# Conditioning product by rows on VectorE in place of partial sums finished on TensorE

## The chip, the cores and the metric

The kernel runs on one core of one Trainium2 chip. The metric is the device time of one execution in microseconds (us). All tensors are float32.

## The reference

The program is a chain of four transformer-like blocks over one sequence of 512 tokens with 1024 features. What matters here is the conditioning ("modulation") of the first two blocks:

```
mod = (silu(c) @ ada_w + ada_b).reshape(bsz, DEPTH, 2, 3, D_MODEL)   # c: 1 x 1024, ada_w: 1024 x 12288
...
shift, scale, gate = (mod[:, i, 0, k][:, None, :] for k in range(3))
h = rmsnorm(x, norm_g[i, 0]) * (1.0 + scale) + shift
y = short_conv_mixer(h, ...)            # i = 0: h @ w_in (1024 x 3072), products, a convolution, @ w_out
x = x + gate * rmsnorm(y, norm_g[i, 1])
shift, scale, gate = (mod[:, i, 1, k][:, None, :] for k in range(3))
h = rmsnorm(x, norm_g[i, 2]) * (1.0 + scale) + shift
y = swiglu_ffn(h, f_w_in[i], f_w_out[i])
x = x + gate * rmsnorm(y, norm_g[i, 3])
```

So `mod` is 12288 numbers, each a dot product of length 1024: 12.6 million multiply-adds over 50 MB of weights. The first 2048 of them (shift and scale of the first norm) are needed before the first large matmul can start.

## The kernel before, in words

Features lie on the 128 partitions, tokens on the free axis: `x` is 8 k tiles of 128 x 512. Every large matmul is done as three float32r products, with the weight chunk `raw` (128 x 1024) split into `whi` (ScalarE, `split_hi`, L1104) and `wlo` (GpSimd, `split_lo`, L518), and the activations into `h_hi` and `h_lo`. A ring of four chunks (`RING = 4`) is loaded by the SyncE queue; SP reloads a slot when `lo_ready` says that its `wlo` is done.

The phases come in program order: `a_in` (24 chunks of 24 matmuls each), `a_out` (8), `f_in0` (44), `f_out0`, then the state-space mixer `m`, `f_in1` and `f_out1` (the same shape of work as `f_in0` and `f_out0`), attention, and a last feed-forward. Each engine runs its own instruction list in the order in which the code is written; semaphores join them.

At the start of a phase, `four` computes the first four output tiles k tile by k tile, so that TensorE can begin as soon as k tile 0 of the normalised input is there (L580 for the two products with `h_hi`, L584 for the one with `h_lo`). All other chunks go through `chunk` (L557).

The normalised input of k tile k is made by three engines. VectorE multiplies `x` by the inverse root, which `spread` has laid over a PSUM bank (`scaled`, L1598, into one of two buffers `ta`; from k = 2 on it waits for the ScalarE work on tile k-2). ScalarE applies scale and shift twice (`norm_out`, L1149 to `h_hi`, L1150 to `tb`). GpSimd, for the last tile VectorE, subtracts (`h_lo`, L533, L1565).

The modulation is made in 24 units of 512 outputs. VectorE adds up, over the 8 k tiles, weight times SiLU(c), with the contraction on the partitions (`mod_unit` L1662 to L1671, `first_part` L1682 to L1687: one `tensor_scalar` and seven `scalar_tensor_tensor` of 128 x 512 each, summed in a PSUM bank, the last one into `modacc` or `acc`). TensorE then sums over the partitions with a column of ones (`modulation` L669, `first_sum` L681 and L685: four float32 matmuls of 128 x 1, which the trace shows as eight), and VectorE adds the bias (`mod_evac` L1654, `first_cols` L1698). Units 0 to 3 are the first stage (`ada_first`). Units 4 to 11 come in `a_in`, one behind each of its eight column groups (`ada_a`), and units 12 to 23 in `f_in0` (`ada_f`). `modulation` stands 20 times in TensorE's list: six times in `a_in`, once in `a_out`, 13 times in `f_in0`.

## Time and profile before

| | |
|---|---|
| median of 3 runs | 2212.21 us (2212.01 to 2213.32) |
| profiled execution, span from first to last instruction | 2209.9 us |
| median less span of the profiled execution | 2.3 us |
| TensorE busy | 2167.0 us, 98% |
| VectorE busy | 1203.4 us, 54% |
| ScalarE busy | 999.4 us, 45% |
| GpSimd busy | 973.0 us, 44% |

No device time of the profiled execution itself is given apart from its span; the other runs last 2.3 us longer than that span. The profile's rows are in microseconds from the start of the span unless marked ns. A row of the timeline gives start, duration, engine, line, operation, and in brackets how long the engine was idle before it and what released it.

### The profile page before, as it was taken

The numbers are of one execution on the slowest core, as the hardware profiler recorded it, in microseconds if no ns is written. First come the engines' busy times: TensorE is split into PE (matmuls) and PEld (weight loads), VectorE is DVE, ScalarE is ACT, GpSimd is POOL, SyncE is SP. The second block draws the span as 40 slices with busy tenths as digits, with TensorE's granted clock in tenths as the row PEclk, the third lists the DMA queues.
The fourth block names the chain that finished last, engine by engine and source line by source line (L and its number), as shares of the span: only waits on it lengthen the run. The fifth ranks groups of instructions, "written<-read, shape, count | busy, mean of one in ns | idle before, by whom it ended". The sixth has DMA issues, their size and how long they took to land.

```text
span 2209.9 us, 29015 instructions
## 1 busy us (share of the span) xinstructions
PE 2167.0 (98%) x10456; PEld 1756.4 (79%) x10456; DVE 1203.4 (54%) x1720; ACT 999.4 (45%) x1425; POOL 973.0 (44%) x421
## 2 busy tenths in 40 slices
PE   7999999999999999999999999999999899999998
PEld 5788888888878777778888888888777688888886
DVE  5877665521176877886522221240888755666522
ACT  4324544334445655654543434453555644444332
POOL 3544444446644333334544456666122143444563
PEclk8999999999999999999999999999999999999999
DMA  7653475553315344333232323344221132333232
GB/s 316 221 209 124 147 272 218 178 161 97 115 58 194 115 148 157 115 124 96 77 95 95 96 74 101 109 122 155 87 70 42 36 105 86 104 95 95 79 97 72
DMA packets 74338, 273.88 MB, mean 124 GB/s; under 512 B 8632, under 2 KB 11320, under 8 KB 67849
## 3 DMA queue, kind: packets, MB, share of 16 engines
q1 hardware_dynamic: 70872, 266.77, 36.5%
q10 hardware_dynamic: 3376, 5.90, 0.8%
q8 instruction: 58, 0.95, 0.2%
q14 instruction: 32, 0.25, 0.0%
HBM read 269.24 MB, written 8.12 MB: 126 GB/s over the span
## 4 chain that ended last, share of the span: by engine, by line
PE 76%; issue 14%; POOL 5%; DVE 3%; ACT 1%; DMA 1%; ACTq 0%; SPq 0%; POOLq 0%; DVEq 0%
PE bank L557 61%; POOL wlo L518 5%; PE bank L974 4%; PE bank L1066 2%; PE bank L580 2%; PE bank L1031 1%; PE bank L995 1%; PE bank L622 1%; PE bank L1014 1%; PE bank L584 1%; PE bank L630 1%; PE bank L669 1%; DMA ada_first<-ada_d 1%; DVE x L1624 1%; PE bank L915 1%
## 5 line engine op out<-in xcount | busy, mean ns | idle before, releaser
L518 POOL TENSOR_TENSOR wlo<-raw,whi 128x1024 fp32r<-128x1024 f32 x382 | 927.6, 2435 | 1146.7 <-ACT whi L1104 1146.4
L1104 ACT ACTIVATE whi<-raw 128x1024 fp32r<-128x1024 f32 x382 | 400.5, 1055 | 560.3 <-PE bank L557 537.8
L557 PE MATMUL bank<-h_hi,whi 128*128 128x512 f32 x1608 | 633.0, 394 | 1.9 <-POOL wlo L518 1.9
L557 PE MATMUL bank<-h_hi,wlo 128*128 128x512 f32 x1608 | 626.5, 390 | 0.0
L557 PE MATMUL bank<-h_lo,whi 128*128 128x512 f32 x1608 | 625.8, 389 | 0.0
L557 PEld LDWEIGHTS bank<-h_hi,whi 128*128 128x128 f32 x1608 | 301.9, 188 | 68.3 <-issue 6.3
L557 PEld LDWEIGHTS bank<-h_hi,wlo 128*128 128x128 f32 x1608 | 301.8, 188 | 64.0
L557 PEld LDWEIGHTS bank<-h_lo,whi 128*128 128x128 f32 x1608 | 302.0, 188 | 61.6
L557 PE MATMUL bank<-g_hi,whi 128*128 128x512 f32 x592 | 230.4, 389 | 0.0
L557 PE MATMUL bank<-g_hi,wlo 128*128 128x512 f32 x592 | 230.3, 389 | 0.0
L557 PE MATMUL bank<-g_lo,whi 128*128 128x512 f32 x592 | 230.3, 389 | 0.0
L1786 DVE TENSOR_TENSOR tb<-ta,bank 128x512 f32<-128x512 f32 x44 | 30.2, 686 | 210.4 <-PE bank L557 193.6
L1565 DVE TENSOR_TENSOR g_lo<-tb,g_hi 128x512 f32 (+1 forms) x52 | 108.3, 2082 | 51.9 <-ACT g_hi L1236 45.0
L557 PEld LDWEIGHTS bank<-g_lo,whi 128*128 128x128 f32 x592 | 111.1, 188 | 23.1
L557 PEld LDWEIGHTS bank<-g_hi,wlo 128*128 128x128 f32 x592 | 111.1, 188 | 23.1
L557 PEld LDWEIGHTS bank<-g_hi,whi 128*128 128x128 f32 x592 | 111.1, 188 | 23.0
L1581 DVE TENSOR_TENSOR sums<-sums,sq 128x512 f32<-128x512 f32 x21 | 14.5, 692 | 186.2 <-ACT sq L1167 186.1
L1724 DVE SCALAR_TENSOR_TENSOR tb<-bank,vec,tb 128x511 f32<-128x511 f32 (+1 forms) x140 | 104.9, 749 | 9.8
L580 PE MATMUL bank<-h_hi,whi 128*128 128x512 f32 x160 | 66.4, 415 | 9.8 <-ACT h_hi L1149 9.8
L533 POOL TENSOR_TENSOR h_lo<-tb,h_hi 128x512 fp32r<-128x512 f32 x35 | 45.2, 1293 | 65.6 <-ACT tb L1150 65.3
L580 PE MATMUL bank<-h_hi,wlo 128*128 128x512 f32 x160 | 65.5, 409 | 0.0
L2156 DVE TENSOR_TENSOR x<-x,bank 128x512 f32<-128x512 f32 x8 | 5.5, 688 | 86.4 <-PE bank L557 86.4
(357 smaller groups left out, 2985.2 us busy)
## 6 DMA issues: line engine op xcount, KB each, us to landing
raw<-f_in_d SPq DMA_DIRECT2D x88, 512.0 KB, 3.5
raw<-m_d SPq DMA_DIRECT2D x65, 512.0 KB, 3.6
ada_f<-ada_d SPq DMA_DIRECT2D x24, 1024.0 KB, 7.0
raw<-g_in_d SPq DMA_DIRECT2D x44, 512.0 KB, 3.5
raw<-w_in_d SPq DMA_DIRECT2D x41, 512.0 KB, 3.6
csb<-cs_d SPq DMA_DIRECT2D x32, 640.0 KB, 6.3
ada_a<-ada_d SPq DMA_DIRECT2D x16, 1024.0 KB, 4.9
raw<-a_in_d SPq DMA_DIRECT2D x24, 512.0 KB, 6.0
```

Source lines behind the costliest of these rows:

```text
L518: nc.gpsimd.tensor_tensor(wlo[:, s], raw[:, s], whi[:, s].bitcast(F32), ALU.subtract).then_inc(lo_ready, 1)
L533: nc.gpsimd.tensor_tensor(h_lo[:, k, :], tb[:, k % 2, :], h_hi[:, k, :].bitcast(F32), ALU.subtract).then_inc(in_ready, 1)
L557: mm = nc.tensor.matmul(psum[bank][:], w[:, s, kk, :], xs[part == "lo"][:, k, :], start=first and kk == 0 and i == 0, stop=last and kk == ...
L580: nc.tensor.matmul(psum[tiles[i]][:], w[:, (C0[name] + i) % RING, k, :], h_hi[:, k, :], start=k == 0 and j == 0, stop=False)
L584: mm = nc.tensor.matmul(psum[tiles[i]][:], whi[:, (C0[name] + i) % RING, k, :], h_lo[:, k, :], start=False, stop=k == KD - 1)
L622: mm = nc.tensor.matmul(psum[bank][:, i:i + 1], src[:, i * P:(i + 1) * P], ones[:, 0:1], start=start and i == 0, stop=False, skip_group_ch ...
L974: mm = nc.tensor.matmul(psum[7][:], w[:, c % RING, m // 3, :], (h_hi, h_lo)[part == "lo"][:, m // 3, :], start=m == 0, stop=m == 23)
L1066: mm = nc.tensor.matmul(psum[b][:], w[:, c % RING, k, :], (h_hi, h_lo)[part == "lo"][:, k, :], start=kk == 0 and i == 0, stop=kk == 3 and ...
L1104: nc.scalar.activation(whi[:, s], raw[:, s], ACT.Copy).then_inc(hi_ready, 1)
L1565: TT(dst, whole, hi.bitcast(F32), ALU.subtract).then_inc(in_ready, 1)
L1724: ins = STT(out=out[:, d:S], in0=src[:, 0:S - d], scalar=col(width - 1 - d), in1=out[:, d:S], op0=ALU.mult, op1=ALU.add)
L1786: TT(tb[:, j % 2, :], ta[:, j % 2, :], psum[b][:], ALU.mult).then_inc(bank_free[b], 1)
```

## The change

The contraction goes to the free axis. `c` is loaded broadcast over all partitions (`cond`, 128 x 1024), ScalarE takes its SiLU into two PSUM banks (`silu_c`, banks 6 and 7), and the weights `ada_w` are stored transposed, so that one partition holds all 1024 weights of one output. One instruction, `tensor_tensor_reduce` over 128 x 1024 (`mod_col`), multiplies, sums, adds the bias and writes one column of `mod`: 128 outputs. A unit is four such instructions. No matmul is left for the modulation. The bytes that are loaded stay the same but for `cond`.

The first stage goes by k tile: shift column k and scale column k, then `scaled(k)`. The mean square of `x` is summed on VectorE (seven additions) in place of eight matmuls with ones. In the SyncE queue the order of the first loads changes, and in ScalarE's list all four `split_hi` of the first ring stand together in front of the first norm. Since banks 6 and 7 are needed by the residual step after `a_out`, the SiLU is made a second time in front of `f_in0` (`condition()`).

```diff
-        acc = sb("acc", [P, S])
-        modacc = sb("modacc", [P, S])
+        cond = sb("cond", [P, 2, S])
+        acc, spare = cond[:, 0, :], cond[:, 1, :]
...
+        silu_c = banks[:, 6:8, :]
...
-                for h in range(2):
-                    dst = ada_first[p][:, 4 * h:4 * h + 4].rearrange("p k n -> p (k n)")
-                    sp.dma_start(dst, io["ada"][2 * p + h]).then_inc(first_in[p][h], 16)
-
-            sp.dma_start(vec[:], io["vec"]).then_inc(vec_in, 16)
+                    sp.dma_start(ring[h].rearrange("p e a n -> p (e a n)"), at(io["ada"], 2 * d + h + it * (2 * n))).then_inc(ada_in[h], 16)
+
+            def ada_start(k):
+                sp.dma_start(ada_first[k].rearrange("p e a n -> p (e a n)"), io["ada"][k]).then_inc(first_in[k], 16)
+
             for h in range(2):
                 sp.dma_start(x[:, 4 * h:4 * h + 4], io["x"].rearrange("p (k n) -> p k n", k=KD)[:, 4 * h:4 * h + 4]).then_inc(x_in[h], 16)
+            sp.dma_start(cond[:].rearrange("p a n -> p (a n)"), io["c"].broadcast_to([P, D])).then_inc(c_in, 16)
+            sp.dma_start(vec[:], io["vec"]).then_inc(vec_in, 16)
+            ada_start(0)
             sp.dma_start(kst[:], io["kst"]).then_inc(kst_in, 16)
-            for v in range(2):
+            load(io["a_in"][0], 0)
+            ada_start(1)
+            for v in range(1, 4):
                 load(io["a_in"][v], v)
-            ada_start(0)
-            for v in range(2, 4):
-                load(io["a_in"][v], v)
-            for p in range(1, 4):
-                ada_start(p)
...
                     turn(k, range(4))
-                    if n == 0 and k % 2 == 0:
-                        first_sum(1 + k // 2)
...
             def first_root():
 
-                for k in range(KD):
-                    pe.wait_ge(sq_out, k + 1)
-                    nc.tensor.matmul(psum[4][:], ones[:], sq[:, k % 2, :], start=k == 0, stop=k == KD - 1).then_inc(row_done, 1)
-                pe.wait_ge(row_out, 1)
-                for i in range(NT):
-                    mm = nc.tensor.matmul(psum[4][:, i:i + 1], rstd[0:1, i * P:(i + 1) * P], ones[0:1, 0:1], start=True, stop=True)
-                mm.then_inc(s_done, 1)
...
-            def modulation(i):
...
+                pe.wait_ge(row_acc, KD - 1)
+                token_sums(4, rstd[:], True).then_inc(s_done, 1)
...
             first_root()
-            first_sum(0)
...
@@ -696,8 +661,6 @@
                 for s in range(3):
                     if 3 * j + s >= 4:
                         single("a_in", 3 * j + s)
-                    if j >= 2 and s == 0:
-                        modulation(2 + j)
                 if j < 3:
 
...
                 single("a_out", u, xs=(g_hi, g_lo))
-                if u == 0:
-                    modulation(10)
             residual_roots(0, sums)
 
             def ffn(n):
-                if n == 0:
-                    four("f_in0", 1)
-                    modulation(11)
+                four(f"f_in{n}", 1 + 2 * n)
+                with pe.Fori(0, 10) as it:
                     for u in range(4, 8):
-                        single("f_in0", u, wait=False)
...
-                    modulation(23)
...
+                        single(f"f_in{n}", u, it, 4, wait=False)
...
-                        act.wait_ge(ncol_ready, k // 2 + 1)
+                        act.wait_ge(ncol_ready, k + 1)
...
 
-            act.wait_ge(vec_in, 16)
-            nc.scalar.activation(csil[:], vec[:, V0["c"]:V0["c"] + KD], ACT.Silu).then_inc(csil_ready, 1)
+            def condition():
+
+                nc.scalar.activation(silu_c, cond[:], ACT.Silu).then_inc(c_ready, 1)
+
             act.wait_ge(const_ready, 1)
+            nc.scalar.activation(root[:, SPARE, 0:1], epscol[:], ACT.Silu)
             for k in range(KD):
                 if k % 4 == 0:
                     act.wait_ge(x_in[k // 4], 16)
-                if k >= 2:
-                    act.wait_ge(row_done, k - 1)
-                nc.scalar.activation(sq[:, k % 2, :], x[:, k, :], ACT.Square).then_inc(sq_out, 1)
-                if k >= KD - 2:
-                    split_hi(k - (KD - 2))
-            act.wait_ge(row_done, KD)
-            nc.scalar.activation(rstd[0:1, :], psum[4][0:1, :], ACT.Copy).then_inc(row_out, 1)
+                if k >= 3:
+                    act.wait_ge(row_acc, k - 2)
+                nc.scalar.activation(sq[:, k % 2, :] if k else rstd[:], x[:, k, :], ACT.Square).then_inc(sq_out, 1)
+            act.wait_ge(c_in, 16)
+            condition()
             set_root()
-            split_hi(2)
-            act.wait_ge(s_ready, 1)
-            take_root(0, ssum[:])
-            split_hi(3)
+            act.wait_ge(s_done, 1)
+            take_root(0, psum[4][:, 0:NT])
+            for c in range(RING):
+                split_hi(c)
+            act.wait_ge(vec_in, 16)
             mod_norm(0, "a_in", 0)
 
...
+            act.wait_ge(ncol_ready, KD + 1)
             mod_norm(1, "f_in0", 1)
+            condition()
...
+            def mod_col(t, src):
+
+                return nc.vector.tensor_tensor_reduce(src, src, silu_c, 1.0, V("ada_b", t), ALU.mult, ALU.add, mod[:, t:t + 1])
+
+            def mod_unit(d, ring):
+
+                for h in range(2):
+                    dve.wait_ge(ada_in[h], 16 * (d - 3))
+                    for e in range(2):
+                        ins = mod_col(4 * d + 2 * h + e, ring[h][:, e])
+                    ins.then_inc((ada_half, mod_part)[h], 1)
+
+            def first_cols(k):
+
+                ins = mod_col(KD + k, ada_first[k][:, 1])
+                ins.then_inc(col_out, 1)
+                dve.wait_ge(col_out, k + 1)
+                ins = STT(out=ncol[:, 0, 0, k:k + 1], in0=mod[:, KD + k:KD + k + 1], scalar=1.0, in1=V("norm_g", k), op0=ALU.add, op1=ALU.mult)
+                ins.then_inc(ncol_ready, 1)
...
+            for k in range(1, KD):
+                dve.wait_ge(sq_out, k + 1)
+                if k >= 2:
+                    dve.wait_ge(row_acc, k - 1)
+                TT(rstd[:], rstd[:], sq[:, k % 2, :], ALU.add).then_inc(row_acc, 1)
...
+            dve.wait_ge(c_ready, 1)
+            for k in range(KD):
+                dve.wait_ge(first_in[k], 16)
+                ins = mod_col(k, ada_first[k][:, 0])
+                if k == 0:
+                    dve.wait_ge(std_out, 1)
+                    nc.vector.tensor_copy(ssum[:], psum[4][:, 0:NT])
                     inverse(0, R1)
+                first_cols(k)
+                if k == 0:
                     dve.wait_ge(rb_done, 1)
...
+                scaled(k, 4, 0, "a_in")
             low("a_in")
...
+                    dve.wait_ge(c_ready, 2)
+                    for j in range(KF):
+                        hidden(j)
+                        if j % 4 < 3 and j < 16:
+                            mod_unit(12 + 3 * (j // 4) + j % 4, ada_f)
+                        if j == 15:
+                            dve.wait_ge(mod_part, 20)
+                            gate_col(1)
+                            for q in range(2, 4):
+                                scale_col(q)
+                                gate_col(q)
...
-    order = [c for p in range(4) for c in (2 * p, 2 * p + 1, 8 + 2 * p, 9 + 2 * p)] + list(range(16, 96))
-    ada = a["ada_w"].reshape(2, KD // 2, P, 96, P)[:, :, :, order]
-    ins["ada"] = ada.reshape(2, KD // 2, P, 24, S).transpose(3, 0, 2, 1, 4).reshape(48, P, KD // 2 * S)
+    ins["c"] = a["c"]
+    order = [t for k in range(KD) for t in (k, KD + k)] + list(range(2 * KD, 96))
+    ins["ada"] = a["ada_w"].T.reshape(96, P, D)[order].reshape(48, 2, P, D).transpose(0, 2, 1, 3).reshape(48, P, 2 * D)
```

Left out are the deleted bodies of `modulation`, `first_sum`, `mod_evac`, `first_part` and the old `mod_unit` and `first_cols`, which the print above has.

What stands in VectorE's list in the first stage, before: from the end of unit 0's partial sum to the middle of unit 1's. `ssum` gets the mean squares, `ta` is the output of `scaled`, and a unit covers two k tiles of shift and scale.

```order
L1687 SCALAR_TENSOR_TENSOR modacc<-ada_first,csil,bank 128x512 [waits dve_step]
L1744 COPY ssum<-bank 128x4 [waits s_done]
L1682 TENSOR_SCALAR bank<-ada_first,csil 128x512 [waits first_in1_0]
L1687 SCALAR_TENSOR_TENSOR bank<-ada_first,csil,bank 128x512 [waits dve_step] x3
L1698 TENSOR_TENSOR mod<-bank,vec 128x2x2 [waits mod_sum,dve_step]
L1702 SCALAR_TENSOR_TENSOR ncol<-mod,vec 128x2 [waits mod_out]
L1570 RECIPROCAL root<-root 128x4 [waits std_out]
L1598 TENSOR_TENSOR ta<-x,bank 128x512 [waits rb_done,r_ready]
L1598 TENSOR_TENSOR ta<-x,bank 128x512
L1687 SCALAR_TENSOR_TENSOR bank<-ada_first,csil,bank 128x512 [waits first_in1_1]
L1687 SCALAR_TENSOR_TENSOR bank<-ada_first,csil,bank 128x512 [waits dve_step] x2
```

In the change, the same place: from the shift column of k tile 0 to `scaled(1)`. The first of each pair of ISA rows is the multiply-and-sum of 128 x 1024, the second writes the sum to one column of `mod` (128 x 1).

```order
L1597 ISA mod 128x1
L1656 COPY ssum<-bank 128x4 [waits std_out]
L1517 RECIPROCAL root<-root 128x4 [waits std_out]
L1597 ISA ada_first,mod<-ada_first,bank,vec 128x1024 [waits r_ready]
L1597 ISA mod 128x1
L1612 SCALAR_TENSOR_TENSOR ncol<-mod,vec 128x1 [waits col_out]
L1545 TENSOR_TENSOR ta<-x,bank 128x512 [waits rb_done]
L1597 ISA ada_first,mod<-ada_first,bank,vec 128x1024 [waits first_in1]
L1597 ISA mod 128x1
L1597 ISA ada_first,mod<-ada_first,bank,vec 128x1024
L1597 ISA mod 128x1
L1612 SCALAR_TENSOR_TENSOR ncol<-mod,vec 128x1 [waits col_out]
```

The eight instructions for two k tiles with a wait for TensorE's sum (`mod_sum`) became two instructions for each k tile with no wait on TensorE, and `scaled` comes once per k tile instead of twice per unit.

ScalarE's list in front of the first norm, before: L1194 squares `x`, L1104 is `split_hi`, L1115 takes the root.

```order
L1104 ACTIVATE whi<-raw 128x1024 [waits raw_in0]
L1194 ACTIVATE sq<-x 128x512 [waits row_done]
L1104 ACTIVATE whi<-raw 128x1024 [waits raw_in1]
L1198 ACTIVATE rstd<-bank 1x512 [waits row_done]
L1119 ACT_TABLE_LOAD
L1119 ACTIVATE root<-epscol 128x1
L1104 ACTIVATE whi<-raw 128x1024 [waits raw_in2]
L1115 ACTIVATE root<-ssum,epscol 128x4 [waits s_ready]
L1104 ACTIVATE whi<-raw 128x1024 [waits raw_in3]
L1149 ACTIVATE h_hi<-ta,mod,ncol 128x512 [waits t_out,ncol_ready]
```

In the change (L1132 is the SiLU of `cond`, L1059 the root, L1048 `split_hi`, L1093 the first `h_hi`):

```order
L1141 ACTIVATE sq<-x 128x512 [waits row_acc] x3
L1132 ACTIVATE bank<-cond 128x1024 [waits c_in]
L1063 ACT_TABLE_LOAD
L1063 ACTIVATE root<-epscol 128x1
L1059 ACTIVATE root<-bank,epscol 128x4 [waits s_done]
L1048 ACTIVATE whi<-raw 128x1024 [waits raw_in0]
L1048 ACTIVATE whi<-raw 128x1024 [waits raw_in1]
L1048 ACTIVATE whi<-raw 128x1024 [waits raw_in2]
L1048 ACTIVATE whi<-raw 128x1024 [waits raw_in3]
L1093 ACTIVATE h_hi<-ta,mod,ncol 128x512 [waits t_out,ncol_ready,vec_in]
```

The splits of chunks 0 and 1 moved behind the squares, and all four splits now stand between the root and the first norm.

SyncE's loads, before:

```order
L384 DMA vec<-vec_d 128x616
L386 DMA x<-x_d 128x2048 x2
L387 DMA kst<-kst_d 128x262
L363 DMA raw<-a_in_d 128x1024 x2
L382 DMA ada_first<-ada_d 128x2048 x2
L363 DMA raw<-a_in_d 128x1024 x2
L382 DMA ada_first<-ada_d 128x2048 x6
L395 DMA dtp<-dtp_d 128x64
```

and in the change:

```order
L380 DMA x<-x_d 128x2048 x2
L381 DMA cond<-c_d 128x1024
L382 DMA vec<-vec_d 128x608
L377 DMA ada_first<-ada_d 128x2048
L384 DMA kst<-kst_d 128x262
L358 DMA raw<-a_in_d 128x1024
L377 DMA ada_first<-ada_d 128x2048
L358 DMA raw<-a_in_d 128x1024
L377 DMA ada_first<-ada_d 128x2048
L358 DMA raw<-a_in_d 128x1024
L377 DMA ada_first<-ada_d 128x2048
L358 DMA raw<-a_in_d 128x1024
L377 DMA ada_first<-ada_d 128x2048 x4
```

Chunk 3 of `raw` was the tenth load, behind two loads of `ada_first` (1024 KB each); now it is the thirteenth, behind four of them and `cond` (512 KB). Before, `vec` is 308 KB, each of the two loads of `x` 1024 KB, `kst` 131 KB and a chunk of `raw` 512 KB.

## Rows read from the trace of the kernel before

**Rows 1.** The page, part 1: busy time, share of span, instructions.

```profile
PE 2167.0 (98%) x10456; PEld 1756.4 (79%) x10456; DVE 1203.4 (54%) x1720; ACT 999.4 (45%) x1425; POOL 973.0 (44%) x421
```

**Rows 2.** What TensorE waited for, whole span: total us, times, longest.

```profile
PE bank L580 <- ACT h_hi L1149: 9.8, 6, 2.1
...
PE bank L669 <- DVE modacc L1671: 1.0, 1, 1.0
```

**Rows 3.** Chain that ended last, a_in: start us, us, what.

```profile
130.12 0.79 PE bank L669 x8
130.90 16.49 PE bank L557 x72
```

**Rows 4.** The same chain at starts and ends of both feed-forwards.

```profile
232.61 3.11 PE bank L580 x8
...
607.26 4.36 PE bank L622 x40
...
1085.72 337.58 PE bank L557 x1488
...
1423.30 4.36 PE bank L622 x40
```

**Rows 5.** TensorE's timeline at the start of f_in1.

```profile
1061.38 0.47 PE L580 MATMUL bank<-h_hi,whi 128*128 128x512 f32 x1 [1.82 <-ACT h_hi L1149]
```

**Rows 6.** The same chain in the first stage.

```profile
6.00 15.85 DMA ada_first<-ada_d
...
28.56 0.82 ACT h_hi L1149
...
29.43 3.78 PE bank L580 x8
33.21 1.71 PE bank L584 x4
...
58.59 0.96 PE bank L708 x2
```

**Rows 7.** Windows: length, busy PE, PEld, DVE, ACT, POOL, clock, DMA share, GB/s.

```profile
10.00:15.00 5.00, 5.00 (x11) 1.72 (x9) 0.42 (x1) 2.87 (x6) 0.00 (x0) 1.00 1.02 430
...
25.00:30.00 5.00, 2.62 (x9) 2.28 (x10) 2.60 (x7) 1.44 (x3) 0.33 (x1) 0.50 1.01 428
```

**Rows 8.** VectorE by group and shape: busy us, mean ns, idle before.

```profile
L1935 DVE TENSOR_TENSOR csb<-csb,cbm 128x1280 f32<-128x1280 f32 x32 | 47.5, 1491 | 4.7 <-ACT cbm L1284 2.2 <-ACT csb L1276 1.6
...
L1898 DVE RECIPROCAL rstd<-rstd 128x512 f32<-128x512 f32 x8 | 26.8, 3345 | 1.9 <-ACT rstd L1292 1.9
...
L1687 DVE SCALAR_TENSOR_TENSOR bank<-ada_first,csil,bank 128x512 f32<-128x512 f32 x22 | 16.6, 755 | 0.7
...
L1761 DVE TENSOR_TENSOR ta<-ta,bank 128x512 f32<-128x512 f32 x8 | 5.4, 681 | 2.8 <-ACT ta L1211 2.8
```

**Rows 9.** VectorE's timeline, two neighbours of a few elements.

```profile
424.32 0.17 DVE L1716 TENSOR_TENSOR ncol<-mod,vec 128x8 f32<-128x8 f32 x1
424.40 0.16 DVE L1709 SCALAR_TENSOR_TENSOR ncol<-mod,vec 128x8 f32<-128x8 f32 x1
```

**Rows 10.** VectorE's timeline, one column group of a_in.

```profile
154.49 0.68 DVE L1761 TENSOR_TENSOR ta<-ta,bank 128x512 f32<-128x512 f32 x1
...
160.93 2.48 DVE L1565 TENSOR_TENSOR g_lo<-tb,g_hi 128x512 fp32r<-128x512 f32 x1 [0.92 <-ACT g_hi L1219]
165.48 0.16 DVE L1654 TENSOR_TENSOR mod<-bank,vec 128x4 f32<-128x4 f32 x1 [2.08 <-PE bank L669]
...
171.76 0.68 DVE L1761 TENSOR_TENSOR ta<-ta,bank 128x512 f32<-128x512 f32 x1
```

**Rows 11.** VectorE's timeline, one tile of f_in0.

```profile
396.47 0.69 DVE L1786 TENSOR_TENSOR tb<-ta,bank 128x512 f32<-128x512 f32 x1 [1.48 <-PE bank L557]
398.22 2.33 DVE L1565 TENSOR_TENSOR g_lo<-tb,g_hi 128x512 f32 x1 [1.06 <-ACT g_hi L1236]
```

**Rows 12.** ScalarE's timeline between f_in0's norm and its first split.

```profile
253.34 1.06 ACT L1104 ACTIVATE whi<-raw 128x1024 fp32r<-128x1024 f32 x1 [2.99 <-PE bank L584]
```

More of the change, by code:

```diff
@@ L174, in program @@
         sums = view(H + 16 * KB, "sums", [P, 3, S])
[L176 to L178 removed]
+        ada_a = [view(at, f"ada_a{i}", [P, 2, 2, S]) for i, at in enumerate((G + 16 * KB, G + 24 * KB))]
+        ada_first = [view(G + 8 * KB * k, f"ada_first{k}", [P, 2, 2, S]) for k in range(KD)]
+        ada_f = [view(at, f"ada_f{i}", [P, 2, 2, S]) for i, at in enumerate((G + 36 * KB, G + 80 * KB))]
         y32 = view(G + 44 * KB, "y32", [P, 16, S])
@@ L203, in program @@
         tbias = [view(at, f"tbias{i}", [P, 2, TB]) for i, at in enumerate((G + 73 * KB, G + 64 * KB))]
-        abias = [t[:].rearrange("p (e w) -> p e w", e=2) for t in (modacc, acc)]
+        abias = [t[:].rearrange("p (e w) -> p e w", e=2) for t in (spare, acc)]
         kc2 = view(G + 73 * KB, "kc2", [P, 2, 2, S])
@@ L707, in _ @@
                     e = min(S, WB + WA - S * j)
[L708 removed]
+                    nc.tensor.matmul(psum[5][0:16, 0:e], tbl[:], hot[:, S * j:S * j + e], start=True, stop=True).then_inc(hot_sum, 1)
             for u in range(KD):
                 single("a_out", u, xs=(g_hi, g_lo))
[L711 to L712 removed]
             residual_roots(0, sums)
             def ffn(n):
[L716 to L718 removed]
+                four(f"f_in{n}", 1 + 2 * n)
+                with pe.Fori(0, 10) as it:
                     for u in range(4, 8):
[L720 to L736 removed]
+                        single(f"f_in{n}", u, it, 4, wait=False)
                 with pe.Fori(0, 2) as it:
@@ L1677, in first_part @@
-            def first_part(p, h):
-                out, half = psum[6 + p % 2][:], KD // 2
-                dve.wait_ge(first_in[p][h], 16)
-                if h == 0:
-                    step(TS(out, ada_first[p][:, 0, :], csil[:, 0:1], None, ALU.mult))
-                elif p >= 2:
-                    dve.wait_ge(mod_sum, p - 1)
-                end = KD if p else DIRECT[0]
-                for k in range(max(1, half * h), min(half * (h + 1), end)):
-                    ins = STT(out=out if k < end - 1 else (modacc, acc)[p % 2][:], in0=ada_first[p][:, k, :], scalar=csil[:, k:k + 1],
-                              in1=out, op0=ALU.mult, op1=ALU.add)
-                    if k < end - 1:
-                        step(ins)
-                if h:
-                    ins.then_inc(mod_part, 1)
@@ L2229, in layout @@
     ins = {}
-    vecs = dict(c=columns(a["c"]), ada_b=columns(a["ada_b"]), norm_g=columns(a["norm_g"]),
+    vecs = dict(ada_b=columns(a["ada_b"]), norm_g=columns(a["norm_g"]),
                 a_conv=taps_columns(a["a_conv_w"][0]),
```

145 lines of the change are left out of this document (19 added, 126 removed).

## The prediction

> **What bounds the kernel now.** I read the page's busy times first: TensorE is busy for 2167.0 of 2209.9 us, and no other engine passes 54% [rows 1]. A busy engine that is pipelined need not be at its peak, so next comes what TensorE waited for. There is almost nothing outside the first stage and attention: 9.8 us in six waits over the whole span for the first tiles of the norms, none longer than 2.1, and one wait of 1.0 us for `modacc` [rows 2]. So from the end of the first stage to the end of `f_out0` (607 us) each microsecond of TensorE's own list is a microsecond of the kernel, and each one off VectorE is worth nothing unless it ends a wait. The chain of waits shows the same in `a_in`: 72 matmuls in 16.49 us, a modulation in 0.79, and so on without a gap [rows 3].
>
> The first stage is the exception. Its chain goes through loads of `ada_first` (one lands at 6.00 + 15.85 = 21.85 us), then VectorE's sums, and the four first tiles start at 29.43 and are over at 58.59 [rows 6]. The 96 matmuls of these tiles need 96 x 0.227 = 21.8 us at the pace of `f_in1` (337.58 us for 1488) [rows 4], so some 37 of these 58.6 us are something else.
>
> **The change part by part.**
>
> *Twenty modulations off TensorE.* In `a_in` a period with one of them is 0.79 + 16.49 = 17.28 us [rows 3]; 72 matmuls at 0.227 us would be 16.34. The difference is 0.94 us: 0.79 for the small matmuls and 0.15 for the change to and from them. Seven of them (six in `a_in`, one in `a_out`) make 6.6 us. For the 13 in `f_in0` the kernel has its own control, since `f_in1` is the same work without modulation. From the first L580 to the residual sums `f_in0` takes 607.26 - 232.61 = 374.65 us, and `f_in1` 1423.30 - 1061.38 = 361.92 [rows 4, 5]. That is 12.7 us, with the wait of 1.0 us for `modacc` in it, and with whatever `f_in1` waits for when no small matmul covers it. Sum: **19.3 us**. Bounds: 18.2, if the change to and from them costs nothing in `a_in` (7 x 0.79 + 12.7), and 19.8 (20 x 0.94 + 1.0).
>
> *The price of one column.* The trace has no multiply-and-sum. VectorE's operations with one operand in PSUM take 681 ns for 512 elements, and a product of 1280 elements takes 1491 ns [rows 8]; that is 1.05 ns for each further element, so 1.22 us for 1024. A second arithmetic step costs no second pass: `scalar_tensor_tensor` of 512 elements takes 755 ns [rows 8]. The write of the sum is an instruction of its own in VectorE's list; its nearest rows are operations of 8 columns, which take 0.17 us but follow each other at 0.08 [rows 9]. I take 1.22 + 0.08 = 1.30 us for a column. The lower bound is 1.15 + 0.08, if neighbours overlap as those of rows 9 do. The upper one, by the nearest row in kind of a slow single instruction, is RECIPROCAL with 3345 ns for 512 elements [rows 8]; between such ends I stay near the additions and products, since the sum is an addition per element, but I keep half rate (2 x 1.07, and 0.15 that does not grow with the size, = 2.3 us, 2.4 with the write) as a case.
>
> The Trainium skill speaks on this point ("Vector Engine (DVE) Microarchitecture Reference", section "Points that are easy to get wrong"): an instruction of the scalar_tensor_tensor layout with an accumulator runs at half throughput when both sources are float32 in SBUF. Here one of them (`silu_c`) is in PSUM, so by its words it would not apply; if it did apply, each column would be about 2.3 us. No row of before shows either.
>
> *Units in `a_in` and `f_in0`.* A unit is now 4 x 1.30 = 5.2 us in place of 171.76 - 165.48 = 6.3 [rows 10]. The rest of a column group in `a_in` is 160.93 + 2.48 - 154.49 = 8.9 us, so VectorE has 14.1 us of work in a period of 16.3 [rows 10, 3]; in `f_in0` a tile is 398.22 + 2.33 - 396.47 = 4.1 us [rows 11] and with a unit 9.3 in 10.9 (48 matmuls). All of it lies beside TensorE's work: 0 us. The cover is gone at 7.4 us a unit in `a_in` (1.8 a column). ScalarE's second SiLU (128 x 1024) costs about what a split of the same size costs, 1.06 us, and stands where ScalarE was idle for 2.99 us [rows 12]: 0 us, at most 1 if more than that came late.
>
> *The first stage.* What is late next? In ScalarE's list all four splits stand ahead of the first norm, and the last one needs chunk 3 of `raw`. Up to it, the queue holds `x` 2048 KB, `cond` 512, `vec` 304, four `ada_first` 4096, `kst` 131 and four chunks 2048: 9139 KB. Before, the load that landed at 21.85 us had 7607 KB up to its end (308 + 2048 + 131 + 4 x 512 + 3 x 1024) [rows 6]. The loads flow at 428 to 430 GB/s from 10 us on [rows 7], so 1532 KB (1.57 MB) more are 3.7 us: chunk 3 lands at **25.5 us**. The squares, seven additions, the SiLU, the root and the columns of k tiles 0 and 1 are done before that (about 21 us: `ada_first` 1 lands near 17, two columns and a `scaled` follow), so they cost nothing; they have some 4 us of cover. Behind the waiting split stand the first norm and thereby `scaled(2)`, which waits for `tb` of tile 0.
>
> Split 3 ends at 26.6. The first `h_hi` takes 0.82 us [rows 6], so TensorE starts at 27.5 in place of 29.43. From there two chains run. TensorE: k tile 0 at the low clock (granted 0.50 of 2.4 GHz, that is 1.2 GHz, as it was when it began before [rows 7]) is 3.78 + 1.71 = 5.5 us [rows 6], the other 84 matmuls 19.1, and 0.5 for the clock's rise: 52.6. VectorE: `tb` of tile 0 is out at 28.2, `scaled(2)` ends at 28.9, and each further k tile is 2 x 1.30 + 0.2 (the scale column's wait and its small operation) + 0.69 = 3.5 us, so `scaled(7)` ends at 46.4. Then come 0.8 + 0.8 us of ScalarE, 0.7 of VectorE's `h_lo` and the last 14 matmuls (3.3): 52.0. The two are within a microsecond of each other, and I take 52.6 against 58.59: **6.0 us** less. Bounds: with columns of 1.23 us TensorE's chain still holds (52.6); with the clock low for one more k tile it is 55; with 1.30 us more per k tile (a collision, below) it is 58.5. An earlier end than 51 would need the clock to rise at once.
>
> Sum: 19.3 + 6.0 = 25.3 us off the span of 2209.9. The median lay 2.3 us above that span, and I expect the same distance: 2212.2 - 25.3 = **2187 us**.
>
> **The rivals.**
>
> *Full forecast* (2187, chance 0.70). Own range 2182 to 2191.
>
> *VectorE's columns collide with GpSimd* (2193, chance 0.12). `h_lo` at 160.93 took 2.48 us [rows 10], while a subtraction of 128 x 512 elements otherwise takes about what the product in rows 8 takes: it waits while GpSimd splits. If a column waited likewise, each k tile of the first stage would gain GpSimd's 1.3 us for its own `h_lo` and end at 58.5, no better than before. In `a_in` a unit could catch one more split (1.8 us): 15.9 of 16.3, still covered. So 19.3 is left: 2193. For it speaks that the instruction writes its whole product to SBUF; against it, that rows of L1687 with a PSUM operand stay at 755 ns while GpSimd works [rows 8]. The Trainium skill ("SBUF — State Buffer", section "Who interferes with whom") has it that an instruction with at most one SBUF input does not contend; L1687's rows agree, for another operation.
>
> *Chunk 3 lands late, or the clock stays low* (2190 to 2192, chance 0.06, taken with the case before in the range). `cond` is a broadcast, 128 times the same 4 KB; each microsecond it takes above its share comes off the 6.0.
>
> *Half rate, which ends on the other side* (2216, chance 0.09). At 2.4 us a column the first stage has k tiles of 5.7 us: 28.9 + 28.5 + 5.6 = 63, or 4.4 us later than now. In `a_in` VectorE needs 8.9 + 9.6 = 18.5 us in 16.3: 2.2 x 8 = 17.6 us. In `f_in0` it is (3 x 13.7 + 4.1) / 4 = 11.3 in 10.9, 0.4 x 16 = 6. Together 28 against 19.3: 9 us slower, or 4 if the first groups are covered by slack, so 2216 to 2221. The sign turns at about 2.2 us a column.
>
> *The matmuls go and nothing is gained* (2206 to 2212, chance 0.03). TensorE would have to wait for something that the small matmuls hid. Against it stands `f_in1`, which runs the same list without them and is 12.7 us shorter.
>
> **How the numbers follow.** What a measurement of this kernel can tell from no change is about 0.2%, 4.4 us. Faster by more: the first three cases and a part of the last, 0.89. Within: 0.04. Slower: nearly all of half rate, 0.07. The range from 2181 to 2198 holds the first three cases with their bounds and leaves out 0.08 above for half rate, 0.03 for nothing gained, and some for a mixture or a faster start.
>
> **What would show it.** TensorE's list without L669 and the chain in `a_in` running 72 matmuls in 16.3 us; `f_in0` as long as `f_in1` within 0.5 us; multiply-and-sum rows of 1.2 to 1.25 us with the write's row at 0.1 to 0.2; the first split of chunk 3 at 25.5 and `h_hi` just behind it; the four tiles over at 52 to 53. The forecast fails if a column is above 1.8 us, if TensorE shows waits behind VectorE or `lo_ready` in `a_in`, or if ScalarE waits for chunk 3 well past 26.

## The result and the profile after

The changed kernel takes **2185.18 us** (median of 4 runs, 2181.89 to 2187.59); the kernel before takes 2212.11 beside it (4 runs, 2211.16 to 2213.32). The ratio is 0.9876, with a 95% interval of 0.9863 to 0.989: 26.9 us less. Run a second time (`e7_again` below) it takes 2184.2 us against 2211.84.

The page's busy times of the profiled execution (span 2180.1 us, its own time 2181.89), to hold against [rows 1]:

```profile
PE 2127.2 (98%) x10232; PEld 1726.8 (79%) x10232; DVE 1194.1 (55%) x1709; ACT 971.6 (45%) x1405; POOL 972.6 (45%) x421
```

TensorE is still the bound, with 224 matmul rows fewer (160 of them are those of the 20 groups), and VectorE is busy for only 9 us less than before. What TensorE waited for (total us, times, longest us), against [rows 2]:

```profile
PE bank L577 <- ACT h_hi L1093: 18.5, 6, 10.7
PE bank L617 <- DVE rstd L1648: 13.2, 1, 13.2
```

The wait for `modacc` is gone. Two long ones stand in its place, both over before 28.6 us, in the first stage: TensorE, which before had small sums to do there, is idle for most of the time until the first `h_hi`. The chain that ended last (start us, us, what), at the places of [rows 3, 4]:

```profile
7.61 19.09 DMA raw<-a_in_d
...
84.01 125.36 PE bank L554 x552
209.37 4.49 PE bank L617 x40
...
243.55 337.57 PE bank L554 x1488
581.12 4.36 PE bank L617 x40
...
1057.29 337.60 PE bank L554 x1488
1394.88 5.48 PE bank L617 x40
```

From 84.01 us on, `a_in` with `a_out` is now one run of 552 matmuls at 0.227 us, and the 1488 of `f_in0` with `f_out0` take 337.57 us, as those of `f_in1` with `f_out1` do to 0.03 us. The same stretches of both kernels, from these rows and those of [rows 4, 6] (end of the four first tiles: 58.59 before; for after the row `53.67 0.96 PE bank L671 x2`):

```
                                    before     after   less
to the end of the four tiles         58.59     53.67    4.9
from there to a_out's sums          162.38    155.70    6.7
a_out's sums to f_out0's sums       386.29    371.75   14.5
f_out0's sums to f_out1's           816.04    813.76    2.3
f_out1's sums to the end            786.6     785.2     1.4
```

The third line has two parts, and the end of `f_in0`'s four first tiles divides them. Before, the first small group follows those tiles at once:

```profile
256.25 0.79 PE bank L669 x8
```

In the changed kernel's timeline, the last matmul of the tiles and the first of the next chunk:

```profile
242.49 0.39 PE L581 MATMUL bank<-h_lo,whi 128*128 128x512 f32 x1
243.55 0.50 PE L554 MATMUL bank<-h_hi,whi 128*128 128x512 f32 x1 [0.67 <-POOL wlo L515]
```

From the end of the tiles to `f_out0`'s sums it was 607.26 - 256.25 = 351.0 us and is now 581.12 - 242.88 = 338.2 (the tiles end at 242.49 + 0.39): **12.8 us** less. The other 1.8 us lie ahead of it, in the norm and the tiles. The last row shows one thing more: where the first of the 13 groups stood, TensorE now waits 0.67 us for GpSimd's `wlo`, so that taking this group away gained only about 0.1 us. The last two lines of the table, and the 1.8, lie where TensorE's matmuls are the same in both kernels: 5.5 us, to which the experiments come back.

The first stage in the timeline of the changed kernel (start us, us, engine, line, operation, out<-in; in brackets the idle time before it and what ended it):

```profile
15.70 1.28 DVE L1597 CUSTOM_DVE_ANT_0 ada_first<-ada_first,bank,vec 128x1024 f32<-128x1024 f32 x1
16.73 2.34 POOL L515 TENSOR_TENSOR wlo<-raw,whi 128x1024 fp32r<-128x1024 f32 x1 [16.28 <-ACT whi L1048]
16.90 0.08 DVE L1597 DVE_READ_ACCUMULATOR2_ANT mod<- 128x1 f32 x1
17.02 2.06 DVE L1612 SCALAR_TENSOR_TENSOR ncol<-mod,vec 128x1 f32<-128x1 f32 x1
19.00 0.68 DVE L1545 TENSOR_TENSOR ta<-x,bank 128x512 f32<-128x512 f32 x1
19.60 1.27 DVE L1597 CUSTOM_DVE_ANT_0 ada_first<-ada_first,bank,vec 128x1024 f32<-128x1024 f32 x1
...
20.80 1.27 DVE L1597 CUSTOM_DVE_ANT_0 ada_first<-ada_first,bank,vec 128x1024 f32<-128x1024 f32 x1
...
26.73 1.06 ACT L1048 ACTIVATE whi<-raw 128x1024 fp32r<-128x1024 f32 x1 [2.68 <-DMA raw<-a_in_d]
27.69 0.80 ACT L1093 ACTIVATE h_hi<-ta,mod,ncol 128x512 fp32r<-128x512 f32 x1
28.55 0.79 PE L577 MATMUL bank<-h_hi,whi 128*128 128x512 f32 x1 [10.69 <-ACT h_hi L1093]
29.23 0.69 DVE L1545 TENSOR_TENSOR ta<-x,bank 128x512 f32<-128x512 f32 x1 [2.74 <-ACT tb L1094]
...
38.61 1.30 POOL L530 TENSOR_TENSOR h_lo<-tb,h_hi 128x512 fp32r<-128x512 f32 x1 [2.30 <-ACT tb L1094]
39.36 0.56 DVE L1612 SCALAR_TENSOR_TENSOR ncol<-mod,vec 128x1 f32<-128x1 f32 x1
```

Read three things here. A column takes 1.27 to 1.28 us and the next starts 1.20 us after it (19.60, 20.80); the write of its sum (0.08) lies in that overlap. ScalarE waits 2.68 us for chunk 3 and then splits it, normalizes, and TensorE starts. And `ncol`, an operation on a single column, takes 2.06 us once and 0.56 us later. Its end is each time the end of what GpSimd does, to 0.02 us: 17.02 + 2.06 = 19.08 and 16.73 + 2.34 = 19.07; 39.36 + 0.56 = 39.92 and 38.61 + 1.30 = 39.91. So it is in all eight. The prediction has no term for it.

### The profile page after: what moved, and what is told of

Its sections match the earlier page's. It is cut to its first block, busy times and chain, and to the rows that moved or that the text cites. A ratio compares the mean times of both kernels' runs of the same rounds, so it can differ in the third digit from the quotient of the medians.

```text
span 2180.1 us, 28310 instructions
## 1 busy us (share of the span) xinstructions
PE 2127.2 (98%) x10232; PEld 1726.8 (79%) x10232; DVE 1194.1 (55%) x1709; ACT 971.6 (45%) x1405; POOL 972.6 (45%) x421
## 4 chain that ended last, share of the span: by engine, by line
PE 74%; issue 14%; POOL 5%; DVE 4%; DMA 1%; ACT 1%; SPq 0%; POOLq 0%; ACTq 0%; DVEq 0%
PE bank L554 62%; POOL wlo L515 5%; PE bank L918 4%; PE bank L1010 2%; PE bank L939 1%; PE bank L975 1%; DVE x L1571 1%; PE bank L617 1%; PE bank L958 1%; DMA raw<-a_in_d 1%; DVE sq L1567 1%; PE bank L625 1%; DVE ada_first L1597 1%; PE bank L859 1%; DVE ta L1545 0%
## 5 line engine op out<-in xcount | busy, mean ns | idle before, releaser
L1048 ACT ACTIVATE whi<-raw 128x1024 fp32r<-128x1024 f32 x382 | 399.8, 1055 | 571.8 <-PE bank L554 549.1
L1512 DVE TENSOR_TENSOR g_lo<-tb,g_hi 128x512 fp32r<-128x512 f32 (+1 forms) x52 | 114.0, 2192 | 48.5 <-ACT g_hi L1183 41.6
L1597 DVE CUSTOM_DVE_ANT_0 ada_f<-ada_f,bank,vec 128x1024 f32<-128x1024 f32 x48 | 59.1, 1275 | 8.5 <-DMA ada_f<-ada_d 8.3
```

Source lines behind the costliest of these rows:

```text
L1048: nc.scalar.activation(whi[:, s], raw[:, s], ACT.Copy).then_inc(hi_ready, 1)
L1512: TT(dst, whole, hi.bitcast(F32), ALU.subtract).then_inc(in_ready, 1)
L1597: return nc.vector.tensor_tensor_reduce(src, src, silu_c, 1.0, V("ada_b", t), ALU.mult, ALU.add, mod[:, t:t + 1])
```

## The experiments

The edits are shown shortened.

### The sums back on TensorE

```
 def column_sums():
+    for b in range(4):
+        matmul(psum[4][:, b:b + 1], rstd[:, b * P:(b + 1) * P], ones[:, 0:1])
+# after single("a_in", ...) for j >= 2, s == 0; a_out u == 0; f_in0: 13 times
```

> The changed kernel with 20 groups of four 1-column matmuls put back on TensorE, with nothing to wait for and no effect on the result: 6 in a_in, 1 in a_out, 13 in f_in0. If the term of 19.3 us is TensorE's time alone, each group costs what it cost before, 0.94 us, with no VectorE work in it: the time is 18 to 20 us above the changed kernel's (some 2204 us), a_in and a_out together 6.6 us longer and f_in0 12.7 us longer than in the changed kernel. Rival: a group cost 0.94 us only through its wait for VectorE's sums; then groups without a wait are cheaper than that, 10 us or less in all.

Measured: 2204.72 us (5 runs, 2203.6 to 2206.49), 19.5 above the changed kernel's first median and 20.5 above its second. The runs of the kernel before beside it had a median of 2214.55, so it is 9.8 us faster than that kernel, where the changed one is 26.9 and 27.6 faster: by this reckoning 17.1 to 17.8 us are lost again. In the profile, a period with one group (its line is 658 there), and the ends of the stretches:

```profile
66.08 5.68 PE bank L554 x24
71.77 0.79 PE bank L658 x8
72.55 11.05 PE bank L554 x48
...
215.43 5.49 PE bank L617 x40
...
248.53 0.79 PE bank L658 x8
...
598.21 5.93 PE bank L617 x40
```

The four tiles end at 53.05, so `a_in` and `a_out` take 162.38 us in place of 155.70: 6.7 us for seven groups, 0.95 each. From the end of `f_in0`'s four tiles, where its first group starts, it is 598.21 - 248.53 = 349.7 us against 338.2: 11.4 for thirteen. The first of them fills the time in which the changed kernel waits for `wlo` and costs 0.1; the other twelve cost 0.94 each. Together 18.1 us, and TensorE's only wait from the end of the first stage to `f_out0`'s sums is one of 1.9 us for `h_hi`, in front of `f_in0`. So the theory holds, at its lower end, and the rival (a cheap group that only waited) falls. The kernel before had 12.8 in the same place: the 1.3 more are in the main the wait of 1.0 us for `modacc` [rows 2], which this run leaves out.

### What holds the first stage: chunk 3, or the small operation

```
 ada_start(0)
-load(a_in 0); ada_start(1); load(a_in 1); ada_start(2); load(a_in 2); ...
+for v in range(4): load(io["a_in"][v], v)
+for k in range(1, KD): ada_start(k)
```

> The changed kernel with the four first chunks of raw queued ahead of modulation columns 1 to 7 instead of between them. Theory: the first h_hi waits for chunk 3 (landed 26.7 us), which is behind 4 MB of columns; with it early, VectorE loses its idle 2.74 us ahead of the third scaled tile and goes at its pace of 3.6 us a k tile from 15.7 us on, so the four tiles are over at about 51.0 us in place of 53.67, 2.7 us less in all. TensorE starts before 23 us but waits for GpSimd's wlo of chunk 3 (about 26.3 us). Rival 1: columns 1 then come too late for VectorE and the gain is under 1 us. Rival 2: TensorE, started early with gaps, has the low clock for longer and the four tiles are over no earlier than 53 us.

Measured: 2184.16 us (4 runs, 2182.83 to 2185.07), no change; the four tiles end at 53.44, 0.2 us earlier than in the changed kernel's first profile. In its second (`e7_again`) they end at 53.13, and in two other runs that have this first stage unchanged at 53.05 and 53.09: what is below 0.6 us here cannot be told from nothing. VectorE and GpSimd in its timeline:

```profile
16.08 9.31 POOL L512 TENSOR_TENSOR wlo<-raw,whi 128x1024 fp32r<-128x1024 f32 x4 [15.63 <-ACT whi L1045]
...
21.13 1.28 DVE L1594 CUSTOM_DVE_ANT_0 ada_first<-ada_first,bank,vec 128x1024 f32<-128x1024 f32 x1 [2.09 <-DMA ada_first<-ada_d]
...
23.66 1.74 DVE L1609 SCALAR_TENSOR_TENSOR ncol<-mod,vec 128x1 f32<-128x1 f32 x1
```

VectorE's idle 2.74 us is gone and 2.09 stand in its place, for the second column pair. With the chunks early, GpSimd splits without a pause from 16.08 to 25.39, and `ncol` waits 1.74 us for it. Rival 1 was right: the columns come late, the wait moved, and the wait for GpSimd took the rest. The end at 53.4 is also what rival 2 forecast, but TensorE's last waits in this stage, from 41 to 50 us, are for `h_hi` and `h_lo`, that is for VectorE's pace, and not a low clock.

```
+step(tensor_copy(psum[5][:, 0:KD], vec[:, norm_g 0:KD]))
-STT(out=ncol[k], in0=mod[8 + k], scalar=1.0, in1=V("norm_g", k), ...)
+STT(out=ncol[k], in0=mod[8 + k], scalar=1.0, in1=psum[5][:, k:k + 1], ...)
```

> The changed kernel with norm_g of the first norm copied to a PSUM bank once, so that the small ncol operation has one of its two sources in PSUM. In the changed kernel each of the eight ncol operations (0.38 to 2.06 us, 128x1) ends within 0.02 us of the end of a GpSimd operation. Theory: an operation with all operands in SBUF does not get through while GpSimd works there, one with a PSUM source does; ncol then takes under 0.2 us each, and VectorE's k tile 3.2 us in place of 3.6. As chunk 3 still lands at 26.7 us, the four tiles are over 1 to 2 us earlier at most (TensorE alone needs 24 us from 28.5: 52.7). Rival: the 0.56 us is the latency of reading the column just accumulated; it stays, and so does the pace of 3.6 us.

Measured: 2183.47 us (4 runs, 2181.92 to 2186.4); the four tiles end at 52.33, 0.7 to 1.3 us earlier than in the profiles of the changed kernel's first stage. In its timeline:

```profile
37.56 1.30 POOL L530 TENSOR_TENSOR h_lo<-tb,h_hi 128x512 fp32r<-128x512 f32 x1 [1.90 <-ACT tb L1094]
38.31 0.16 DVE L1612 SCALAR_TENSOR_TENSOR ncol<-mod,bank 128x1 f32<-128x1 f32 x1
```

The same operation, reading the same fresh column, takes 0.16 us in the middle of a GpSimd operation. The latency rival falls. VectorE's k tile goes from 3.59 to 3.19 us. As expected little of it shows in the end, since chunk 3 still holds the start (VectorE is now idle for 4.79 us ahead of its third `scaled`).

> Both edits together, chunks first and norm_g in PSUM. Theory: with chunk 3 out of the way the VectorE pace binds, so the edits add more than alone: k tile pace 3.2 us from 15.7 us, scaled(7) over at about 41 us; TensorE, which waits for GpSimd's wlo of chunk 3 until 26.3 us, needs about 22 us from there: four tiles over at 48 to 50 us, 4 to 5.5 us less than in the changed kernel. Rival: GpSimd (2.35 us for each wlo, 1.3 for each h_lo) or the low clock holds TensorE back and the four tiles are over at 51 us or later, no better than chunks first alone.

Measured: **2180.19 us** (4 runs, 2179.05 to 2183.05), ratio to the kernel before 0.9847 (0.9827 to 0.9867). The four tiles end at 49.43, 4.2 us before those of the changed kernel's first profile (3.6 to 4.2 by all of them), where the single edits gave 0.2 and 1.3 by the same measure. Two rows of its timeline:

```profile
16.03 9.33 POOL L512 TENSOR_TENSOR wlo<-raw,whi 128x1024 fp32r<-128x1024 f32 x4 [15.58 <-ACT whi L1045]
...
25.42 0.79 PE L574 MATMUL bank<-h_hi,whi 128*128 128x512 f32 x1 [1.11 <-POOL wlo L512]
```

From 25.42 us on TensorE has no wait until the four tiles are over: it is GpSimd's four `wlo` that now set the start, and TensorE the end. `scaled(7)` ends at 43.5 us, 2.5 later than forecast, because the second column pair still comes late (VectorE is idle for 3.13 us before it), but that no longer sets the end. The theory held in its sum (48 to 50 us), and this is the fastest version that was run.

### Both sources of a column in SBUF

```
-silu_c = banks[:, 6:8, :]
+silu_c = cond[:]                 # SiLU written in place, the second condition() left out
```

> The changed kernel with SiLU(c) kept in SBUF (written over the condition, once) in place of two PSUM banks, so that both sources of a column's multiply-and-sum are float32 in SBUF; everything else as before. By the Trainium skill (Vector Engine (DVE) Microarchitecture Reference, Points that are easy to get wrong) the instruction then runs at half throughput. Theory: a column takes 2.1 to 2.4 us in place of 1.20, even while GpSimd is idle, and it also waits for a running GpSimd operation as ncol did; the first stage takes some 10 us more, a_in and f_in0 20 to 25 us more as VectorE becomes their bound: 2215 to 2225 us. Rival: throughput stays at 1.2 us while GpSimd is idle and only the waits for GpSimd appear; then the first stage loses 5 us or less and a_in and f_in0 stay covered: 2185 to 2192 us.

Measured: 2196.22 us (4 runs, 2196.04 to 2196.47), 11 to 12 above the changed kernel. In its timeline:

```profile
20.55 3.35 DVE L1596 CUSTOM_DVE_ANT_0 ada_first<-ada_first,cond,vec 128x1024 f32<-128x1024 f32 x1
...
37.55 1.27 DVE L1596 CUSTOM_DVE_ANT_0 ada_first<-ada_first,cond,vec 128x1024 f32<-128x1024 f32 x1
38.75 1.28 DVE L1596 CUSTOM_DVE_ANT_0 ada_first<-ada_first,cond,vec 128x1024 f32<-128x1024 f32 x1
39.31 1.87 POOL L530 TENSOR_TENSOR h_lo<-tb,h_hi 128x512 fp32r<-128x512 f32 x1 [2.29 <-ACT tb L1094]
```

Neither forecast has the time right, and the mechanism is the rival's. The throughput does not change: with GpSimd idle a column is 1.27 us and the next starts after 1.20, the same as with a PSUM source. A column that starts while GpSimd works takes 3.35 us, since it waits for the end of that operation (19.96 to 22.81 here); and an operation of GpSimd that starts during a column is itself longer (1.87 in place of 1.30). The 32 columns of the units in `a_in` take 2478 ns in the mean (1275 to 3443). The rival priced these waits too low, but the cost is far from the theory's 30 us: the four tiles end at about 60.2 us (6.5 later), `a_in` with `a_out` takes 160.5 us (4.8 more), and `f_in0` 337.58, nothing more at all. The Trainium skill ("Vector Engine (DVE) Microarchitecture Reference", section "Points that are easy to get wrong") has half throughput for the scalar_tensor_tensor layout with two sources in SBUF that are not bf16. No row tells whether this instruction, which the profile shows as a custom one, has that layout; it shows no halving (1.28 us against 1.28). The Trainium skill's "SBUF — State Buffer", section "Who interferes with whom", has the rest: a VectorE instruction with two SBUF inputs contends with GpSimd's reads, whoever issues first is served first, and one with a single SBUF input does not contend unless it runs in a two-port mode. The 3.35, 0.56 and 0.16 us agree.

### How much VectorE could still take

```
 for e in range(2):
+    step(mod_col(4 * d + 2 * h + e, ring[h][:, e]))
     ins = mod_col(4 * d + 2 * h + e, ring[h][:, e])
```

> The changed kernel with every column of the 20 units in a_in and f_in0 computed twice in a row (the second time from the product that the first left in the loaded weights, so the later modulation values are not the reference's); first stage unchanged. This is what half rate would have cost outside the first stage. By the recorded arithmetic a unit of 9.6 us on 8.9 of other work is 18.5 us in a period of 16.3, 2.2 us too much in each of 8 periods, and 0.4 us in each of 16 in f_in0: 24 us, so some 2209 us. Rival: the four PSUM banks and VectorE's own idle time between dependent steps are worth less than that sum assumes, and VectorE's waits add to the work: 35 us or more. Rival on the other side: the periods smooth each other out and it costs under 10.

Measured: 2190.53 us (4 runs, 2189.37 to 2192.38), 5 to 6 us above the changed kernel where 24 were expected: the rival on the other side. Two periods of VectorE in `a_in`, each from a unit's first column to the next unit's (most rows left out):

```profile
76.61 1.27 DVE L1597 CUSTOM_DVE_ANT_0 ada_a<-ada_a,bank,vec 128x1024 f32<-128x1024 f32 x1
...
91.53 1.27 DVE L1597 CUSTOM_DVE_ANT_0 ada_a<-ada_a,bank,vec 128x1024 f32<-128x1024 f32 x1
...
101.64 0.68 DVE L1670 TENSOR_TENSOR ta<-ta,bank 128x512 f32<-128x512 f32 x1
102.36 1.58 DVE L1633 TENSOR_SCALAR tb<-ta,vec 128x512 f32<-128x512 f32 x1
103.97 1.54 DVE L1635 SCALAR_TENSOR_TENSOR tb<-ta,vec,tb 128x511 f32<-128x511 f32 x2
105.55 0.69 DVE L1675 TENSOR_TENSOR tb<-tb,bank 128x512 f32<-128x512 f32 x1
106.94 0.69 DVE L1512 TENSOR_TENSOR g_lo<-tb,g_hi 128x512 fp32r<-128x512 f32 x1 [0.70 <-ACT g_hi L1165]
107.55 1.27 DVE L1597 CUSTOM_DVE_ANT_0 ada_a<-ada_a,bank,vec 128x1024 f32<-128x1024 f32 x1
```

The unit is 10.1 us long and everything else 4.8 and 5.9, so the periods are 14.9 and 16.0 us. All seven are between 14.9 and 17.2, 15.9 in the mean, below TensorE's 16.3. The difference is L1633, which takes 0.49 us in the first period and 1.58 in the second, where it lies beside a split of GpSimd's; it has one tensor in SBUF as its input, so a single input in SBUF is no safeguard for every VectorE operation. In the changed kernel the same rest takes more: its two steps of the convolution (3.62 us at 112.81) and `g_lo` (2.48) lie beside GpSimd's splits and wait for them, and here they fall elsewhere (1.54 and 0.69). So the 8.9 us that the prediction took for VectorE's other work were some 5 of work and 4 of waiting, and waiting gives way. `f_in0` takes 337.58 us: nothing. The 4.8 us sit in `a_in` and `a_out` (160.5 from the four tiles' end to the sums): 2.9 are one wait of TensorE for the last `g_lo` before `a_out`, which ends at 172.96, and the rest is the slower start after it (its matmuls follow each other at 0.43 us, with a granted clock of 0.50 to 175 us).

> The changed kernel with 6 columns in place of 4 in each of the 20 units of a_in and f_in0 (the first of each half twice, with the same remark on the values). A unit is then about 7.3 us, just under the 7.4 at which the recorded arithmetic has the cover of a_in gone. Theory: no change that can be measured (within 3 us of the changed kernel), a_in and a_out within 1 us of their 155.7 us. Rival: VectorE's waits inside its period (for ScalarE and TensorE, about 2 us in a_in) count as work; then the cover ends near 6.9 us a unit and a_in and f_in0 grow by 0.4 us a period or more, 6 us or more in all.

Its edit repeats the first column of each half only. Measured: 2184.66 us (4 runs, 2183.97 to 2186.76), and the four tiles' end to `a_out`'s sums 155.70 us (53.09 to 208.79), as in the changed kernel: no cost.

### The changed kernel again

> The changed kernel itself, once more, on this chip and beside the runs of the kernel before. The 26.9 us between the first medians is 2.7 more than the 24.2 that the stages account for (19.3 and 4.9). Theory: the rest is how long the low clock lasts around each set of residual sums, which differs from run to run: the difference to before will be anything from 22 to 30 us, and the spans will follow the mean clock, about 1.1 us for each 0.001. Rival: the rest is a real gain of the change elsewhere; then the difference is 26 to 28 us again.

Measured: 2184.2 us (5 runs, 2183.15 to 2186.81) against 2211.84 (9 runs, 2206.74 to 2214.9), ratio 0.9883 (0.9867 to 0.99): 27.6 us. That number lies in both forecasts and decides nothing alone. Its first stage ends at 53.13 us, 5.5 before that of the kernel before. Its spans go from 2181.3 us at a mean clock of 0.990 to 2185.0 at 0.988; the first four from 2180.1 at 0.992 to 2185.8 at 0.987: 1.1 to 1.9 us for each 0.001. Windows of 24 us from `f_out0`'s sums on, where the residual leaves TensorE gaps (us; PE, PEld, DVE, ACT, POOL busy; granted clock; DMA share; GB/s). Of the kernel before:

```profile
607.26:631.26 24.00, 22.08 (x109) 18.85 (x108) 20.12 (x33) 13.91 (x20) 10.30 (x8) 0.79 0.14 45
```

Of the changed kernel:

```profile
581.12:605.12 24.00, 22.12 (x118) 19.21 (x118) 19.99 (x33) 13.75 (x20) 10.34 (x8) 0.93 0.16 45
```

Of `e1_sums_back`:

```profile
598.21:622.21 24.00, 22.12 (x104) 19.51 (x105) 18.36 (x31) 12.43 (x18) 9.30 (x8) 0.79 0.14 45
```

In all ten profiles the granted clock is below full in this window, from 0.72 to 0.93. In the kernel before it is at its lower level (0.50, that is 1.2 GHz) from 615 to 620 us, where TensorE is busy for 3.15 of the 5 us. How long that lasts differs between executions of the same code. Over the profiles of all ten kernels, the stretch from `f_out0`'s sums to the next ones (581.12 to 1023.22 in the changed kernel), where the code is the same in all, takes 441.9 to 446.0 us, and 444.4 in the kernel before; from `f_out1`'s sums to the end it is 784.1 to 789.0, and 786.6 before. The kernel before lies inside both ranges. From `a_out`'s sums to the end of `f_in0`'s tiles it is 31.7 to 35.3 us, and 35.3 before. The three kinds of stretch together (all that lies behind `a_out`'s sums except `f_in0`'s matmuls with `f_out0`) are 1632.5 to 1638.7 us in the nine profiles of changed kernels, and 1637.9 before; the changed kernel's first profile, with 1632.5, is the shortest. So the 5.5 us of the first comparison need no cause in the change.

## Why the prediction was right

The forecast was 2187 us, with 2182 to 2191 as the range of the full forecast and 2181 to 2198 over all; the time is 2185.2. Step by step:

**Twenty sums off TensorE: right, in place and size.** 19.3 us forecast; the rows of after give 6.7 + 12.8 = 19.5. The sums put back, without their wait for `modacc`, cost 18.1 in rows and 17 to 20.5 in the medians. What made this good was to take `f_in1` as the control for `f_in0`: the 1488 matmuls of the two now differ by 0.03 us. That it came out to 0.2 us has some luck in it, since the stretch that the prediction subtracted, from the first matmul of the tiles to the sums, now takes 361.9 us in `f_in0` and 360.4 in `f_in1`; the sign "within 0.5 us" was missed by that measure, through the clock in the first tiles.

**The price of one column: right to a tenth.** 1.22 us forecast for the operation, 1.27 measured; 0.08 for the write, 0.08 measured. Adding the two was the mistake: the write lies in the overlap and the pace is 1.20, below the lower bound of 1.23.

**Units hidden: right, with more cover than was said.** No wait of TensorE for VectorE appears from the end of the first tiles to `a_out`'s sums, nor in `f_in0` behind its norm. The second SiLU cost 2.3 us (a table load of 1.28 stands in front of it) in place of 1.06, and was covered too. But "the cover is gone at 7.4 us a unit" is wrong: 7.3 us a unit cost nothing (so far in line), and about 10 cost 5 us where the recorded sum gives 24. The 8.9 us of other work was read from rows that held waits for GpSimd. By the same step the half-rate rival was priced too high outside the first stage, since `e6_eight_columns` has VectorE busy outside it for as long as half rate would: 19.5 - 5 there, less the prediction's own 4.4 for the first stage, is an estimate of 10 us faster than before. So the sign turns above 2.4 us a column; where, no run shows.

**First stage: right mechanism, mis-sized: 4.9 us (5.5 in `e7_again`) in place of 6.0.** Three of its numbers moved. Chunk 3 lands at 26.7 and not 25.5 (26.2 to 26.3 in six other runs with the same order of loads): the flow was taken as 428 GB/s, and the window of 8 to 12 us, with `cond` in it, shows 370 where the kernel before had 423. That is 0.5 us; the rest of the delay has no single place. TensorE's own chain would have been over at 28.55 + 4.7 (its slow first k tile, 5.5 in the forecast) + 19.1 = 52.4, close to the 52.6 forecast, though it started 1 us later: the first tile was shorter, and the 0.5 us for the clock's rise has no row. But it was VectorE's chain that ended last. `scaled(7)` ends at 47.7 in place of 46.4, and the matmuls behind it at 53.67. In VectorE's k tile of 3.5 us two errors cancel: columns 0.2 us cheaper in all, `ncol` 0.4 us dearer (3.59 measured). `e3_g_in_psum` shows that the latter is the wait for GpSimd.

**The rivals.** *Collision with GpSimd* did happen, but to `ncol` and not to the columns: they take 1272 to 1275 ns in the mean, beside a working GpSimd too, and `e5_silu_in_sbuf` shows that the PSUM source is why. *Chunk 3 late* happened too, by 0.7 to 1.2 us. *Half rate* did not, and no run here shows it even with both sources in SBUF. *Nothing gained* is excluded by the first experiment.

**Median and span.** The difference of the medians (26.9, then 27.6) is 2.5 and 2.7 us above what the two terms measure in the rows, 24.4 with the first profile and 24.9 with the second. `e1_sums_back`, whose TensorE list differs from that of the kernel before only in the first stage, is 9.8 us faster than the runs of that kernel beside it, or 7.4 against its first median, where the rows give 58.59 - 53.05 = 5.5 for the first stage and 1.3 in `f_in0`. The runs of the kernel before spread from 2206.7 to 2218.8 us, and the stretches that are the same in all kernels by 6 us, so these 2.5 us are within the spread. Whether they are luck or a longer low clock that belongs to the old first stage stays open. With the rows' 24.4 us alone the median would have been 2187.7.

## What to carry to other kernels

When one stage of a tuned kernel exists twice, with and without the thing to be removed, the difference of the two is the best price there is. A busy time of VectorE beside a working GpSimd is work plus waiting; before you call an engine's cover used up, look at how long the same rows take elsewhere. And where two waits stand one behind the other (a load, then GpSimd), removing either gives little, 0.2 and 1.3 us here, and both together 4.2.
